# First layer of a hybrid decoder step: another order of the projections, key rows taken earlier, and masks applied by predicated copies

## The chip, the cores and the metric

The kernel runs on one core of one Trainium2 chip, in fp32 throughout. The metric is device time in microseconds (us). A core has five engines that work side by side, each through its own list of instructions in order: TensorE (PE, with its weight loads shown as PEld), VectorE (DVE), ScalarE (ACT), GpSimd (POOL) and SyncE (SP), which here only issues the loads of weights. They wait for one another on semaphores. An instruction that waits holds up everything behind it on its own engine, and this is what the change is about.

## The reference, cut to what matters

The model has two layers and runs for a prompt of 512 tokens and for 8 samples of 4 tokens each; the kernel handles all 544 tokens together. Only the mixer of the first layer is touched by the change:

```python
u = xn @ w_in
q_a, k_a, v_a, g_a, gk_lr, q_b, f_b, i_b, g_b = split(u)
log_alpha = log_sigmoid(gk_lr @ w_gk2 + b_gk) / 16
o_a, _ = chunk_gated_linear(q_a * DK_A ** -0.5, k_a, v_a, log_alpha, s_gla)
log_f = logaddexp(log(max(lb, 1e-20)), log1p(-lb) + log_sigmoid(f_b))
k_b = (1 - lb) * sigmoid(-f_b)
o_b, _ = chunk_gated_linear(silu(q_b) * N_B ** -0.5, k_b, i_b, log_f, s_hgrn)
# in chunk_gated_linear, by chunks of 64 tokens: b = cumsum(log_g)
scores[t, s] = sum_c q[t, c] * k[s, c] * exp(b[t, c] - b[s, c])   # for s <= t
```

Heads 0 to 3 ("a") have 64 key columns and heads 4 to 7 ("b") have 128. Two "a" heads share a tile of 128 rows, so keys, queries and decays make up six tiles: tile 0 and 1 (a pair of "a" heads each), tiles 2 to 5 (one "b" head each).

## The kernel before, in words

**Units.** The projection `xn @ w_in` is computed in 29 units of 128 output columns each (`even_units`, L590), in the order f_b (4 units), gk (1), k_a (2), q_a (2), q_b (4), v_a (4), i_b (4), g_a (4), g_b (4). The text numbers them in the order in which they run, unit 0 to unit 28. A unit is 48 matmuls of 128 x 272 (L328): each fp32 weight is split into a rounded part (w_head) and the rest (w_rest), and each input also, and three of the four products are formed. Units go alternately to slab 0 and slab 1 (two weight buffers, each with its PSUM banks, 0 and 1 or 2 and 3). gk has one unit only, on slab 0, and the unit that follows it is on slab 0 as well.

**Feeding a unit.** SP loads 512 KB of raw weights into a slab (L277), and waits before each load until the slab's earlier rest has been taken (rest_ok). ACT makes w_head (L292) when the load has landed and the slab's previous unit is done (`act_head`), and DVE makes w_rest (L297, `dve_rest`). The helper `ahead` puts the head and the rest of the next unit of the same slab right behind the end of a unit, in ACT's and DVE's lists. SP issues loads strictly in the order of the stages. Before the first norm, ACT and DVE split one slab for each of slab 0 and slab 1, written out by hand in the list `todo` (near L2412), ahead of `norm_part(norm0)`. In the norm, ACT squares eight tiles (L506) and DVE adds them (L534, L537).

**What runs beside the units.** All four engines walk through the units, and after the unit's own work a fixed piece of the decay and score work is written into each engine's list by unit number. `dve_decay` and `act_decay` are chains of steps that yield (logarithms, exponentials, running sums L752 `scan`). `steps_after` says how many of the 36 factor steps are taken after a unit (six tiles, levels 1 to 6): for each, POOL subtracts (L804, L805), ACT takes the exponential (L883), DVE multiplies by keys and queries (L830, L831). There are two buffers for these, so POOL runs at most two steps ahead of DVE. `job_after` says after which unit PE computes a head's scores (`pe_scores`, L913 for the prompt, L918 for the samples): seven levels, and level n waits for factor step n of its tile. Jobs 0 to 7 stand after units 13, 14, 17, 18, 20, 22, 24 and 26.

**Masks.** `masked` on DVE multiplies each level's scores in PSUM by its 0/1 mask and adds the levels up (L848, L853, L856 and, for the samples, L860, L864, L867: 11 instructions for a head). The next job on PE waits for the multiplications, as they free the banks.

**Value rows.** After units 13 to 20, PE transposes the values that the unit made (L620, L621). These transposes stand in the middle of the following unit, and ACT waits for them, copies them out (L643, L645) and only then takes the factor steps of its unit.

**The end.** For each of the six tiles, POOL forms differences to the chunk's last token (L815), ACT two exponentials (L888, L889) and DVE four instructions (L873 to L876, `dve_ends`). All six stand after units 27 and 28, three after each. PE then transposes each tile of keys into rows (L936, L937, `key_rows_even`): three after unit 28 and three at the head of `pe_chunks`, and ACT copies them (L1007, L1009). Behind that come the chunk recurrence (L954 to L969) and the samples' part (L987, L998).

Of the kernel before, what the change touches and what calls it, by code (L numbers as in the profile page):

```python
# [16 lines left out]
F32R = mybir.dt.float32r  # L17
ACT = mybir.ActivationFunctionType
ALU = mybir.AluOpType
# [133 lines left out]
def trunk(nc, a, o, known, seen, stop=99):  # L153
    ctx = ExitStack()
    with ctx:
# [59 lines left out]
        for name, n in (("f_b", 2), ("gk", 1), ("k_a", 1), ("q_a", 1), ("q_b", 2), ("v_a", 2), ("i_b", 2), ("g_a", 2),  # L215
                        ("g_b", 2)):
# [161 lines left out]
        pT = cols(34 * T + 5 * D + 5 * KTILES * P, 8, 5, CE)  # L378
        qk = cols(0, LEVELS, T)
        ee = soft[:, 0:2, :]  # L380
        mt = cols(LEVELS * T, 2, 512)
# [6 lines left out]
        lbs = cols(34 * T + 5 * D + 5 * KTILES * P + 2500, 40)  # L388
# [9 lines left out]
        lvmask = tab[:, 0:7 * CE].rearrange("p (l t) -> p l t", l=7)  # L398
# [177 lines left out]
        def norm_part(n):  # L576
# [3 lines left out]
        norm0 = Norm("mix0", lambda k: col("norm_mix", k), "f_b")  # L580
# [10 lines left out]
                      ("f_b", "gk", "k_a", "q_a", "q_b", "v_a", "i_b", "g_a", "g_b")  # L591
                      for i in range(stages[name][0]) for s in range(len(stages[name][1]))]
        value_tile = {u: u - 13 for u in range(13, 21)}
        job_after = {13: 0, 14: 1, 17: 2, 18: 3, 20: 4, 22: 5, 24: 6, 26: 7}
        steps_after = {10: 2, 11: 2, 12: 2, 15: 3, 16: 3, 18: 1, 19: 5, 20: 1, 21: 5, 22: 1, 23: 5, 24: 1, 25: 5}

        def pe_even_in(pe):
            for u, (name, i, s, last) in enumerate(even_units):
                between = (lambda: value_rows(pe, u - 1)) if u - 1 in value_tile else None
                unit_products(pe, name, i, s, tile_ready(norm0) if u == 0 else None, between=between)  # L600
                if u == 5:
# [9 lines left out]
                if u == 28:  # L611
                    for j in range(3):
                        key_rows_even(pe, j)
# [9 lines left out]
        def act_even_in(act):  # L623
            act.dma_start(wgk2[0:16, :], a["w_gk2"][0]).then_inc(*E1.dma.loaded("wgk2"))
            decay, exps = act_decay(act), act_scores(act)
            for u, (name, i, s, last) in enumerate(even_units):
# [12 lines left out]
                if u in (1, 3, 6, 7, 10, 12, 13, 14):  # L639
# [9 lines left out]
                if u >= 27:  # L649
                    for kt in range(3 * (u - 27), 3 * (u - 27) + 3):  # L650
                        act_ends(act, kt)

        def dve_even_in(dve):
            decay, factor = dve_decay(dve), dve_factors(dve)
            for u, (name, i, s, last) in enumerate(even_units):
# [9 lines left out]
                if u == 5:  # L665
# [4 lines left out]
                if u in (0, 2, 5, 8, 9, 10, 11, 14, 15, 16, 17, 19):  # L670
                    next(decay)
                if u in job_after and u != 26:
# [3 lines left out]
                if u == 26:  # L676
                    masked(dve, job_after[u])
                if u >= 27:
                    for kt in range(3 * (u - 27), 3 * (u - 27) + 3):
                        dve_ends(dve, kt)  # L680
# [6 lines left out]
        zz = lg[:, :, :]  # L687
        hz = lg[:, 2:6, :]

        def dve_decay(dve):  # L690
# [11 lines left out]
            step(dve.tensor_scalar(lb_om, lb, -1.0, 1.0, ALU.mult, ALU.add), "lbo")  # L702
            yield
            for s in range(2):
                dve.wait_ge(bank_free[s], used["k_a"][s])
            dve.wait_ge(*E1.dve.at("z1"))
            step(dve.scalar_tensor_tensor(out=soft, in0=zz, scalar=-1.0, in1=zz, op0=ALU.mult, op1=ALU.max), "abs")
            yield
            dve.wait_ge(*E2.act.at("ln"))
            step(dve.scalar_tensor_tensor(out=soft, in0=zz, scalar=0.0, in1=soft, op0=ALU.min, op1=ALU.subtract), "lsig")  # L710
            yield
            step(dve.tensor_scalar(lg[:, 0:2, :], soft[:, 0:2, :], 1.0 / 16.0, None, ALU.mult), "gla")
            for kt in range(2):
                scan(dve, kt)
            step(dve.tensor_tensor(kk[:, 2:6, :], soft[:, 2:6, :], hz, ALU.subtract), "kz")
            yield
# [15 lines left out]
            for t in range(4):  # L732
                dve.scalar_tensor_tensor(out=lg[:, 2 + t, :], in0=lg[:, 2 + t, :], scalar=lb_c[:, t:t + 1],
                                         in1=soft[:, 2 + t, :], op0=ALU.max, op1=ALU.add).then_inc(
                    *E2.dve.done(f"lf{t}"))
            yield
# [4 lines left out]
            scan(dve, 2)  # L741
            yield
            dve.wait_ge(*E2.act.at("qs"))
            dve.tensor_scalar(qq[:, 2:6, :], qq[:, 2:6, :], NBK ** -0.5, None, ALU.mult).then_inc(*E2.dve.done("qb"))
            for kt in range(3, KTILES):
                scan(dve, kt)
                yield
# [7 lines left out]
        def act_decay(act):  # L755
# [5 lines left out]
            act.activation(lb_1m, lb_om, ACT.Ln).then_inc(*E2.act.done("l1m"))  # L761
            yield
            act.wait_ge(*E2.dve.at("abs"))
            act.activation(soft, soft, ACT.Exp, scale=-1.0).then_inc(*E2.act.done("e"))
            yield
            act.wait_ge(*E2.act.at("e"))
            act.activation(soft, soft, ACT.Ln, bias=1.0).then_inc(*E2.act.done("ln"))
# [6 lines left out]
            yield  # L774
# [19 lines left out]
        def pool_scores(pool):  # L794

            for n, (kt, level) in enumerate(steps):
# [8 lines left out]
                pool.tensor_tensor(e[:, :, 1, :], b[:, :, 1, :], mid, ALU.subtract).then_inc(*E3.pool.done(f"e{n}"))  # L805

            for kt in range(KTILES):
                b, e = lg[:, kt, :], ee[:, kt % 2, :]
                if kt >= 2:
                    pool.wait_ge(*E3.dve.at(f"kh{kt - 2}"))  # L810
                else:
                    pool.wait_ge(*E3.dve.at(f"qk{len(steps) - 2 + kt}"))
                for lo, n, c in ((0, NCE, CE), (TP, NB, ST)):
                    bb = b[:, lo:lo + n * c].rearrange("p (n c) -> p n c", c=c)
                    ins = pool.tensor_tensor(e[:, lo:lo + n * c].rearrange("p (n c) -> p n c", c=c),  # L815
                                             bb[:, :, c - 1:c].to_broadcast([P, n, c]), bb, ALU.subtract)
                ins.then_inc(*E3.pool.done(f"eh{kt}"))

        def dve_factors(dve):
            for s in range(2):  # L820
                dve.wait_ge(bank_free[s], used["q_b"][s])
# [13 lines left out]
        def masked(dve, j):  # L835

            h = jobs[j][1]
            b0 = 4
            dve.wait_ge(*E3.pe.at(f"g{h}"))
            if j > 0:  # L840
                dve.wait_ge(*E3.dve.at(f"ps{jobs[j - 1][1]}"))
            for q in range(4):
                nl = 2 if q < 3 else 1
                out = mt[:, 1, 0:nl * 256] if q else mt[:, 0, 0:512]
                m = lvmask[:, 2 * q:2 * q + nl, :].unsqueeze(2).to_broadcast([P, nl, 4, CE])
                if q > 1:
                    dve.wait_ge(*E3.dve.at(f"a{h}_{q - 1}"))
                dve.tensor_tensor(out.rearrange("p (l c t) -> p l c t", l=nl, c=4),  # L848
                                  ps[:, b0 + q, 0:nl * 256].rearrange("p (l c t) -> p l c t", l=nl, c=4), m,
                                  ALU.mult).then_inc(*E3.dve.done(f"m{h}_{q}"))  # L850
                if q > 0:
                    dve.wait_ge(*E3.dve.at(f"m{h}_{q}"))
                    dve.tensor_tensor(mt[:, 0, 0:nl * 256], mt[:, 0, 0:nl * 256], out, ALU.add).then_inc(  # L853
                        *E3.dve.done(f"a{h}_{q}"))
            dve.wait_ge(*E3.dve.at(f"a{h}_3"))
            dve.tensor_tensor(pT[:, h, 0:4, :], mt[:, 0, 0:256].rearrange("p (c t) -> p c t", c=4),  # L856
                              mt[:, 0, 256:512].rearrange("p (c t) -> p c t", c=4), ALU.add).then_inc(
                *E3.dve.done(f"p{h}"))

            dve.tensor_tensor(mt[0:TS, 1, 0:96].rearrange("p (l t) -> p l t", l=3),  # L860
                              ps[0:TS, b0 + 3, 256:352].rearrange("p (l t) -> p l t", l=3),
                              lvmask[0:TS, 0:3, 0:TS], ALU.mult).then_inc(*E3.dve.done(f"s{h}"))
            dve.wait_ge(*E3.dve.at(f"s{h}"))
            dve.tensor_tensor(mt[0:TS, 1, 0:32], mt[0:TS, 1, 0:32], mt[0:TS, 1, 32:64], ALU.add).then_inc(  # L864
                *E3.dve.done(f"s2{h}"))
            dve.wait_ge(*E3.dve.at(f"s2{h}"))
            dve.tensor_tensor(pT[0:TS, h, 4, 0:TS], mt[0:TS, 1, 0:32], mt[0:TS, 1, 64:96], ALU.add).then_inc(  # L867
                *E3.dve.done(f"ps{h}"))

        def dve_ends(dve, kt):  # L870
            b, e = lg[:, kt, :], ee[:, kt % 2, :]
# [14 lines left out]
        def act_ends(act, kt):  # L886
            act.wait_ge(*E3.pool.at(f"eh{kt}"))
            act.activation(ee[:, kt % 2, :], ee[:, kt % 2, :], ACT.Exp)  # L888
            act.activation(lg[:, kt, :], lg[:, kt, :], ACT.Exp).then_inc(*E3.act.done(f"eq{kt}"))  # L889

        def pe_scores(pe, j):
# [3 lines left out]
            if j == 0:  # L895
                pe.wait_ge(*E1.dve.at("z1"))
                for s in range(2):
                    pe.wait_ge(bank_free[s], used["q_b"][s])
# [3 lines left out]
            for level in range(LEVELS + 1):  # L902
                left = kk[r0:r0 + dk, kt, :] if level == 0 else qk[r0:r0 + dk, level - 1, :]
                right = qq[r0:r0 + dk, kt, :] if level == 0 else left
                if j > 0 and level % 2 == 0:
                    pe.wait_ge(*E3.dve.at(f"m{jobs[j - 1][1]}_{level // 2}"))
                if j > 0 and level == 0:
                    pe.wait_ge(*E3.dve.at(f"s{jobs[j - 1][1]}"))
# [7 lines left out]
                if level <= 2:  # L916
                    at = 256 + 32 * level
                    pe.matmul(ps[0:TS, b0 + 3, at:at + TS], left[:, TP:T], right[:, TP:T], start=True, stop=True)  # L918
# [8 lines left out]
        def key_rows_even(pe, j):  # L927
# [3 lines left out]
            if j < 2:  # L931
                pe.wait_ge(*E3.dve.at(f"ps{HA + HB - 1}"))
# [6 lines left out]
        def pe_chunks(pe):  # L939
            for j in range(3, KTILES):  # L940
                key_rows_even(pe, j)
# [60 lines left out]

        def act_chunks(act):
            for j in range(KTILES):
                b0 = 4 + 2 * (j % 2)
                act.wait_ge(*E4.pe.at(f"kt{j}"))
# [1492 lines left out]
```

## Time and profile before

| | us |
|---|---|
| median of 3 runs (2268.4 to 2269.01) | 2269.0 |
| the profiled execution, its own time | 2277.18 |
| its span, first to last instruction | 2275.2 |
| PE busy | 1958.6 (86%) |
| DVE busy | 991.6 (44%) |
| ACT busy | 747.1 (33%) |
| POOL busy | 158.2 (7%) |

The span is what the profiler sees between the first and the last instruction; the execution's own time is 1.98 us longer, and the unprofiled median is 8.2 us shorter than that. Busy shares are averages over the whole span. In the profile's rows the clock column (PEclk) is TensorE's granted clock as a share of 2.4 GHz: 1.00 is 2.4 GHz, 0.50 is 1.2 GHz. Times in rows count from the span's start.

### The profile page before, as it was taken

The page shows a single profiled execution, that of the slowest core. Times are in us where ns is not written, and L with a number is a line of the kernel's source. Part 1 is how long each engine was busy: PE and PEld are TensorE (multiplying, and loading weights), DVE is VectorE, ACT ScalarE, POOL GpSimd, SP SyncE. Part 2 cuts the span into 40 slices and gives each one's busy share as a digit, 9 for nine tenths or more (in the row PEclk, how much of TensorE's full clock was granted, in tenths as well). Part 3 has the DMA queues.
Part 4 walks back from the last instruction along what each step waited for, and adds up shares of the span by engine and source line. Part 5 has one row for each costly group of instructions (what it writes and reads, how often), then busy time and mean ns, then how long its engine had stood idle before and what let it go on. Part 6 is the DMA issues. An engine that isn't in the chain of part 4 may idle for free.

```text
span 2275.2 us, 48233 instructions
## 1 busy us (share of the span) xinstructions
PE 1958.6 (86%) x21197; PEld 1818.7 (80%) x21197; DVE 991.6 (44%) x1359; ACT 747.1 (33%) x963; POOL 158.2 (7%) x159
## 2 busy tenths in 40 slices
PE   4999989787999999896898867678578999999987
PEld 4998978577999999793787756666358899999976
DVE  5477721344332333547488433323453433323343
ACT  3353320344541222322365121111362442222233
POOL 1043521101000000100000000000100100000010
PEclk8999955588999999997899866755559999999988
DMA  3221220212232233120122200001202223233211
GB/s 99 75 66 48 66 65 8 56 47 91 86 97 79 77 89 99 51 84 19 56 66 57 66 4 4 4 18 27 42 0 74 93 83 100 67 92 90 86 56 49
DMA packets 237103, 138.60 MB, mean 61 GB/s; under 512 B 6561, under 2 KB 232161, under 8 KB 236945
## 3 DMA queue, kind: packets, MB, share of 16 engines
q1 hardware_dynamic: 226528, 114.31, 17.4%
q0 software_dynamic: 4048, 13.67, 2.4%
q10 hardware_dynamic: 6368, 8.22, 1.1%
q8 instruction: 135, 2.21, 0.4%
q14 instruction: 24, 0.19, 0.0%
HBM read 128.02 MB, written 8.16 MB: 60 GB/s over the span
## 4 chain that ended last, share of the span: by engine, by line
PE 76%; DVE 13%; ACT 5%; issue 4%; DMA 1%; POOL 1%; ACTq 0%; DVEq 0%; POOLq 0%
PE ps L328 55%; PE ps L1906 1%; PE ps L1900 1%; DVE mix L527 1%; DVE x_split L547 1%; PE ps L998 1%; PE ps L969 1%; PE ps L959 1%; PE ps L954 1%; PE ps L987 1%; PE ps L1328 1%; ACT w_head L292 1%; PE ps L1526 1%; PE ps L2067 1%; DVE x_split L1577 1%
## 5 line engine op out<-in xcount | busy, mean ns | idle before, releaser
L328 PE MATMUL ps<-x_split,w_head 128*128 128x272 f32 (+1 forms) x5568 | 953.4, 294 | 73.7 <-DVE x_split L547 41.1
L328 PEld LDWEIGHTS ps<-x_split,w_head 128*128 128x128 f32 x5568 | 807.5, 193 | 96.3 <-issue 69.0
L328 PE MATMUL ps<-x_split,w_rest 128*128 128x272 f32 (+1 forms) x2784 | 585.3, 292 | 0.0
L292 ACT ACTIVATE w_head<-w_raw 128x1024 fp32r<-128x1024 f32 (+1 forms) x206 | 228.4, 1109 | 704.8 <-PE ps L328 697.0
L328 PEld LDWEIGHTS ps<-x_split,w_rest 128*128 128x128 f32 x2784 | 446.2, 193 | 0.0
L297 DVE TENSOR_TENSOR w_rest<-w_raw,w_head 128x1024 fp32r<-128x1024 f32 (+1 forms) x206 | 268.2, 1302 | 398.8 <-ACT w_head L292 398.7
L328 PE MATMUL ps<-hidden_split,w_head 128*128 128x272 f32 x1408 | 233.1, 287 | 0.0
L328 PEld LDWEIGHTS ps<-hidden_split,w_head 128*128 128x128 f32 x1408 | 198.0, 188 | 0.0
L328 PE MATMUL ps<-hidden_split,w_rest 128*128 128x272 f32 x704 | 145.2, 287 | 0.0
L1180 DVE TENSOR_TENSOR hT<-hT,ps 128x544 f32 (+1 forms) x48 | 34.7, 722 | 207.9 <-PE ps L328 207.9
L527 POOL TENSOR_TENSOR mix<-hT,mix 128x544 f32<-128x544 f32 x20 | 36.8, 1842 | 1098.6 <-ACT mix L511 1078.2
L328 PEld LDWEIGHTS ps<-hidden_split,w_rest 128*128 128x128 f32 x704 | 110.0, 188 | 0.0
L1296 DVE TENSOR_TENSOR mix<-mix,ps 128x544 f32<-128x544 f32 x44 | 31.8, 723 | 132.1 <-PE ps L328 132.1
L292 ACT ACT_TABLE_LOAD x21 | 26.9, 1283 | 92.5 <-PE ps L328 82.1
L1900 PE MATMUL ps<-odd_quad 32*32 32x32 f32 x2080 | 31.8, 228 | 15.6 <-DVE odd_quad L2024 8.5
L1900 PEld LDWEIGHTS ps<-odd_quad 32*32 32x32 f32 x2080 | 28.7, 141 | 19.6 <-issue 9.5
L804 POOL TENSOR_TENSOR mix<-mix 128x256 f32<-128x256 f32 (+1 forms) x36 | 32.4, 899 | 158.3 <-DVE mix L831 89.5
L913 PE MATMUL ps<-mix 64*64 64x64 f32 (+1 forms) x896 | 36.7, 229 | 7.6 <-DVE mix L831 7.6
L527 DVE TENSOR_TENSOR mix<-hT,mix 128x544 f32<-128x544 f32 x20 | 30.1, 1525 | 26.2 <-ACT mix L511 25.8
L913 PEld LDWEIGHTS ps<-mix 64*64 64x64 f32 (+1 forms) x896 | 30.9, 140 | 11.2 <-DVE mix L831 8.7
L497 DVE TENSOR_TENSOR mix<-mix 128x544 f32<-128x544 f32 x48 | 34.5, 720 | 11.2 <-ACT mix L491 11.2
L517 ACT ACTIVATE x_split<-mix,vectors 128x544 fp32r<-128x544 f32 x40 | 28.3, 744 | 33.2 <-POOL mix L527 28.8
(361 smaller groups left out, 2235.2 us busy)
## 6 DMA issues: line engine op xcount, KB each, us to landing
w_raw<-in_w_ffn_gate SPq DMA_DIRECT2D x44, 512.0 KB, 3.8
w_raw<-in_w_ffn_up SPq DMA_DIRECT2D x44, 512.0 KB, 3.8
w_raw<-in_w_ffn_down SPq DMA_DIRECT2D x32, 704.0 KB, 4.4
w_raw<-in_w_in_even SPq DMA_DIRECT2D x29, 512.0 KB, 3.8
w_raw<-in_w_ple_gate SPq DMA_DIRECT2D x16, 512.0 KB, 3.7
w_raw<-in_w_out_even SPq DMA_DIRECT2D x8, 512.0 KB, 3.7
w_raw<-in_rw_wr SPq DMA_DIRECT2D x8, 512.0 KB, 3.6
w_raw<-in_rw_wk SPq DMA_DIRECT2D x8, 512.0 KB, 3.7
```

The costliest lines, as they stand in the source:

```text
L292: act.activation(wh[:, s, 0:kt * P], raw[:, s, 0:kt * P], ACT.Copy).then_inc(head_ok[s], 1)
L297: dve.tensor_tensor(wl[:, s, 0:kt * P], raw[:, s, 0:kt * P], wh[:, s, 0:kt * P].bitcast(F32), ALU.subtract).then_inc(rest_ok[s], 1)
L328: mm = pe.matmul(ps[:, 2 * s + h, 0:half.stop - half.start], w[:, s, k * P:(k + 1) * P], x[:, k, half], start=first and k == 0, stop=k == ...
L497: dve.tensor_tensor(n.sum, n.sum, n.sq[:, s, :], ALU.add).then_inc(sum_ok, 1)
L517: act.activation(xh[:, k, :], n.y[:, k % 3, :], ACT.Copy, scale=n.gain(k)).then_inc(*s.act.done(f"h{k}"))
L527: eng.tensor_tensor(n.y[:, k % 3, :], hT[:, k, :], n.rs, ALU.mult).then_inc(*signal.done(f"y{k}"))
L547: dve.scalar_tensor_tensor(out=xl[:, k, :], in0=n.y[:, k % 3, :], scalar=n.gain(k), in1=xh[:, k, :].bitcast(F32), op0=ALU.mult, op1=ALU.su ...
L804: pool.tensor_tensor(e[:, :, 0, :], mid, b[:, :, 0, :], ALU.subtract)
L913: mm = pe.matmul(ps[64 * (c % 2):64 * (c % 2) + CE, b0 + level // 2, at:at + CE], left[:, c * CE:(c + 1) * CE], right[:, c * CE:(c + 1) * CE],
L1180: dve.tensor_tensor(h, h, out2(s), ALU.add).then_inc(bank_free[s], 1)
L1296: dve.tensor_tensor(two(prod), two(act_out), out2(1), ALU.mult).then_inc(prod_ok, 1)
L1900: mm = pe.matmul(at_block(out, p, g, j, i), at_block(bT, p, g, j, i), at_block(xx, p, g, j, i), start=True, stop=True)
```

## The change

The new order of the stages is gk, k_a, q_a, f_b, q_b, and from there as before. The first two tiles' decay is computed on its own, ahead of the "b" decays; the lists by unit number are rewritten; the work of the end stands in the lists of earlier units, in buffers of its own (`ends`); key rows are transposed after units 23, 24 and 25. The masks become integers, and ten predicated copies write a head's scores into pT, which POOL sets to zero once.

```diff
@@ stages and even_units @@
-        for name, n in (("f_b", 2), ("gk", 1), ("k_a", 1), ("q_a", 1), ("q_b", 2), ("v_a", 2), ...
+        for name, n in (("gk", 1), ("k_a", 1), ("q_a", 1), ("f_b", 2), ("q_b", 2), ("v_a", 2), ...
@@ buffers @@
+        ends = soft[:, 2:4, :]
-        mt = cols(LEVELS * T, 2, 512)
-        lvmask = tab[:, 0:7 * CE].rearrange("p (l t) -> p l t", l=7)
+        lvmask = tab.bitcast(I32)[:, 0:7 * CE].rearrange("p (l t) -> p l t", l=7)
@@ lists by unit @@
-        job_after = {13: 0, 14: 1, 17: 2, 18: 3, 20: 4, 22: 5, 24: 6, 26: 7}
-        steps_after = {10: 2, 11: 2, 12: 2, 15: 3, 16: 3, 18: 1, 19: 5, 20: 1, 21: 5, 22: 1, 23: 5, 24: 1, 25: 5}
+        job_after = {6: 0, 7: 1, 10: 2, 11: 3, 15: 4, 17: 5, 19: 6, 21: 7}
+        ends_after = {15: 0, 17: 1, 19: 2, 21: 3, 22: 4, 23: 5}
+        steps_after = {4: 2, 5: 4, 7: 1, 8: 2, 9: 3, 13: 2, 14: 4, 15: 1, 16: 5, 17: 1, 18: 5, 19: 1, 20: 5}
+        keys_after = {23: (0, 1), 24: (2, 3), 25: (4, 5)}
@@ pieces of act_decay and dve_decay, by unit @@
-                if u in (1, 3, 6, 7, 10, 12, 13, 14):            # ACT
+                if u in (1, 3, 9, 11, 12, 13):
-                if u in (0, 2, 5, 8, 9, 10, 11, 14, 15, 16, 17, 19):   # DVE
+                if u in (0, 2, 3, 4, 8, 10, 11, 12, 13, 14, 15, 17):   # and 9, behind its factor steps
@@ dve_decay: the first pair alone, in the pieces of units 2, 3, 4 @@
+            dve.wait_ge(*E1.dve.at("z1"))
+            step(dve.scalar_tensor_tensor(out=soft[:, 0:2, :], in0=gz, ...), "absg")
+            yield
+            dve.wait_ge(*E2.act.at("lng"))
+            step(dve.scalar_tensor_tensor(out=soft[:, 0:2, :], in0=gz, ...), "lsigg")
+            step(dve.tensor_scalar(gz, soft[:, 0:2, :], 1.0 / 16.0, None, ALU.mult), "gla")
+            scan(dve, 0)
+            yield
+            scan(dve, 1)
@@ act_decay, in the piece of unit 3 @@
+            act.activation(soft[:, 0:2, :], soft[:, 0:2, :], ACT.Exp, scale=-1.0).then_inc(*E2.act.done("eg"))
+            act.wait_ge(*E2.act.at("eg"))
+            act.activation(soft[:, 0:2, :], soft[:, 0:2, :], ACT.Ln, bias=1.0).then_inc(*E2.act.done("lng"))
@@ pool_scores @@
+            pool.memset(pT_flat, 0.0).then_inc(*E3.pool.done("zero"))
...
+                if level == LEVELS and kt >= 2:
+                    pool_ends(pool, kt - 2)
@@ masked @@
+            for level in range(3):
+                dve.copy_predicated(pT[0:TS, h, 4, 0:TS], lvmask[0:TS, level, 0:TS], ps[0:TS, 7, at:at + TS])
+            for level in range(LEVELS + 1):
+                dve.copy_predicated(pT[:, h, 0:4, :], lvmask[:, level, :].unsqueeze(1).to_broadcast([P, 4, CE]),
+                                    ps[:, 4 + level // 2, at:at + 256].rearrange("p (c t) -> p c t", c=4))
@@ pe_scores @@
-                if level <= 2:
-                    pe.matmul(ps[0:TS, b0 + 3, at:at + TS], left[:, TP:T], right[:, TP:T], start=True, stop=True)
+            for level in range(3):
+                mm = pe.matmul(ps[0:TS, b0 + 3, at:at + TS], left, right, start=True, stop=True)
@@ todo, ahead of the first norm @@
-            dict(scalar=lambda e: [act_head(e, "f_b", s, 0) for s in range(2)],
-                 vector=lambda e: [dve_rest(e, "f_b", s, 0) for s in range(2)]),
+            dict(scalar=lambda e: [act_head(e, "gk", 0, 0), act_head(e, "k_a", 1, 0)],
+                 vector=lambda e: [dve_rest(e, "gk", 0, 0), dve_rest(e, "k_a", 1, 0)]),
```

## Rows read from the trace of the kernel before

**Rows 1.** Stretches: the units, then the gap before the chunks

```profile
core 0: us, PE busy (x) PEld busy (x) DVE busy (x) ACT busy (x) POOL busy (x), PEclk, DMA share, GB/s
39.79:282.94 243.15, 230.18 (x2379) 222.15 (x2379) 162.72 (x247) 95.75 (x127) 72.84 (x81) 0.95 0.23 62
282.94:298.06 15.12, 5.85 (x33) 4.55 (x31) 10.38 (x20) 10.07 (x23) 12.04 (x15) 0.67 0.53 135
```

**Rows 2.** The chain in order of time: start, length, what

```profile
21.45 2.36 DVE w_rest L297 x2
...
48.10 25.09 PE ps L328 x198
```

**Rows 3.** SP's loads in order of time

```profile
22.70 0.37 SPq L277 DMA_DIRECT2D w_raw<-in_w_in_even  x1
63.62 0.99 SPq L277 DMA_DIRECT2D w_raw<-in_w_in_even  x2
```

**Rows 4.** What PE waited for, 50 to 300: total, times, longest

```profile
PE ps L936 <- DVE mix L873: 8.2, 1, 8.2
PE ps L913 <- DVE mix L831: 7.6, 8, 1.7
PE ps L328 <- DVE w_rest L297: 3.0, 1, 3.0
```

**Rows 5.** What PE waited for, 216 to 283 (jobs 5 to 7)

```profile
PE ps L913 <- DVE mix L831: 2.9, 3, 1.2
```

**Rows 6.** ACT in order of time (in brackets: idle before)

```profile
69.31 1.06 ACT L292 ACTIVATE w_head<-w_raw 128x1024 fp32r<-128x1024 f32 x1 [6.97 <-DMA w_raw<-in_w_in_even]
...
99.37 1.28 ACT L767 ACT_TABLE_LOAD   x1
...
119.14 2.02 ACT L770 ACTIVATE mix<-mix 128x2176 f32<-128x2176 f32 x1
```

**Rows 7.** DVE in order of time: decay steps, masks of job 0

```profile
113.87 2.48 DVE L752 TENSOR_TENSOR_SCAN mix<-tables,mix 128x544 f32<-128x544 f32 x2
116.27 2.80 DVE L715 TENSOR_TENSOR mix<-mix 128x2176 f32<-128x2176 f32 x1
...
120.57 2.50 DVE L719 TENSOR_SCALAR mix<-mix 128x544 f32<-128x544 f32 x4
...
140.25 1.28 DVE L848 TENSOR_TENSOR mix<-ps,tables 128x512 f32<-128x512 f32 x2
...
143.74 0.42 DVE L848 TENSOR_TENSOR mix<-ps,tables 128x256 f32<-128x256 f32 x1
...
145.49 0.18 DVE L867 TENSOR_TENSOR mix<-mix 32x32 f32<-32x32 f32 x1
```

**Rows 8.** POOL in order of time: the first factor step, its second half

```profile
116.75 2.83 POOL L805 TENSOR_TENSOR mix<-mix 128x272 f32<-128x272 f32 x1
```

**Rows 9.** PE in order of time: scores of jobs 3 and 4

```profile
189.91 0.68 PE L913 MATMUL ps<-mix 64*64 64x64 f32 x16
...
192.27 2.08 PE L913 MATMUL ps<-mix 64*64 64x64 f32 x64
207.61 0.69 PE L913 MATMUL ps<-mix 128*64 128x64 f32 x16
...
214.68 0.69 PE L913 MATMUL ps<-mix 128*64 128x64 f32 x16 [1.71 <-DVE mix L831]
```

**Rows 10.** ACT in order of time: value rows, then factor steps

```profile
205.46 0.60 ACT L643 ACTIVATE mix<-ps 128x512 f32<-128x512 f32 x1 [2.73 <-PE ps L621]
...
206.11 1.17 ACT L883 ACTIVATE mix<-mix 128x544 f32<-128x544 f32 x2
```

**Rows 11.** Stretches behind jobs 0 and 4, then the chunk stage

```profile
137.80:144.70 6.90, 6.88 (x53) 6.57 (x54) 6.47 (x11) 4.45 (x4) 3.63 (x4) 0.51 0.47 131
...
216.20:219.80 3.60, 3.60 (x18) 3.60 (x18) 3.46 (x7) 0.00 (x0) 0.64 (x1) 0.53 0.52 146
304.50:377.50 73.00, 71.27 (x336) 66.13 (x336) 11.48 (x42) 4.78 (x8) 0.00 (x0) 0.50 0.00 1
377.50:438.00 60.50, 57.56 (x184) 41.23 (x184) 14.68 (x12) 4.79 (x6) 17.59 (x14) 0.50 0.22 59
```

More of the change, by code:

```diff
@@ L214, in trunk @@
         X = (xh, xl)
-        for name, n in (("f_b", 2), ("gk", 1), ("k_a", 1), ("q_a", 1), ("q_b", 2), ("v_a", 2), ("i_b", 2), ("g_a", 2),
+        for name, n in (("gk", 1), ("k_a", 1), ("q_a", 1), ("f_b", 2), ("q_b", 2), ("v_a", 2), ("i_b", 2), ("g_a", 2),
                         ("g_b", 2)):
@@ L610, in pe_even_in @@
                     pe_scores(pe, job_after[u])
-                if u == 28:
-                    for j in range(3):
-                        key_rows_even(pe, j)
+                for j in keys_after.get(u, ()):
+                    key_rows_even(pe, j)
         def value_rows(pe, u):
@@ L648, in act_even_in @@
                     next(exps)
-                if u >= 27:
-                    for kt in range(3 * (u - 27), 3 * (u - 27) + 3):
-                        act_ends(act, kt)
+                if u in ends_after:
+                    act_ends(act, ends_after[u])
+                for j in keys_after.get(u, ()):
+                    act_key_rows(act, j)
         def dve_even_in(dve):
@@ L675, in dve_even_in @@
                     next(factor)
[L676 to L680, printed above, removed]
+                if u == 9:
+                    next(decay)
+                if u in ends_after:
+                    dve_ends(dve, ends_after[u])
         gam = vec[:, 0, VCOL["hgrn_gamma"][1]:VCOL["hgrn_gamma"][1] + 4]
         lb_e, lb_r, lb_sm, lb, lb_c, lb_1m, lb_om, lb_t = (lbs[:, 4 * i:4 * i + 4] for i in range(8))
-        zz = lg[:, :, :]
+        gz = lg[:, 0:2, :]
         hz = lg[:, 2:6, :]
@@ L735, in dve_decay @@
                     *E2.dve.done(f"lf{t}"))
+            scan(dve, 2)
             yield
@@ L740, in dve_decay @@
                     *E2.dve.done(f"kb{t}"))
-            scan(dve, 2)
-            yield
             dve.wait_ge(*E2.act.at("qs"))
             dve.tensor_scalar(qq[:, 2:6, :], qq[:, 2:6, :], NBK ** -0.5, None, ALU.mult).then_inc(*E2.dve.done("qb"))
-            for kt in range(3, KTILES):
-                scan(dve, kt)
-                yield
+            yield
+            scan(dve, 3)
+            yield
+            scan(dve, 4)
+            yield
+            scan(dve, 5)
+            yield
         def scan(dve, kt):
@@ L837, in masked @@
             h = jobs[j][1]
-            b0 = 4
             dve.wait_ge(*E3.pe.at(f"g{h}"))
[L840 to L854, printed above, removed]
@@ L863, in masked @@
[L863 to L868, printed above, removed]
+            if j == 0:
+                dve.wait_ge(*E3.pool.at("zero"))
+            for level in range(3):
+                at = 256 + 32 * level
+                if level > 0:
+                    dve.wait_ge(*E3.dve.at(f"s{h}_{level - 1}"))
+                dve.copy_predicated(pT[0:TS, h, 4, 0:TS], lvmask[0:TS, level, 0:TS],
+                                    ps[0:TS, 7, at:at + TS]).then_inc(
+                    *E3.dve.done(f"s{h}_{level}"))
@@ L870, in dve_ends @@
+            for level in range(LEVELS + 1):
+                at = (level % 2) * 256
+                if level > 0:
+                    dve.wait_ge(*E3.dve.at(f"m{h}_{level - 1}"))
+                dve.copy_predicated(pT[:, h, 0:4, :], lvmask[:, level, :].unsqueeze(1).to_broadcast([P, 4, CE]),
+                                    ps[:, 4 + level // 2, at:at + 256].rearrange("p (c t) -> p c t", c=4)).then_inc(
+                    *E3.dve.done(f"m{h}_{level}"))
         def dve_ends(dve, kt):
-            b, e = lg[:, kt, :], ee[:, kt % 2, :]
+            b, e = lg[:, kt, :], ends[:, kt % 2, :]
@@ L887, in act_ends @@
             act.wait_ge(*E3.pool.at(f"eh{kt}"))
-            act.activation(ee[:, kt % 2, :], ee[:, kt % 2, :], ACT.Exp)
+            act.activation(ends[:, kt % 2, :], ends[:, kt % 2, :], ACT.Exp)
             act.activation(lg[:, kt, :], lg[:, kt, :], ACT.Exp).then_inc(*E3.act.done(f"eq{kt}"))
@@ L905, in pe_scores @@
                 if j > 0 and level % 2 == 0:
-                    pe.wait_ge(*E3.dve.at(f"m{jobs[j - 1][1]}_{level // 2}"))
-                if j > 0 and level == 0:
-                    pe.wait_ge(*E3.dve.at(f"s{jobs[j - 1][1]}"))
+                    pe.wait_ge(*E3.dve.at(f"m{jobs[j - 1][1]}_{min(level + 1, LEVELS)}"))
                 if level:
@@ L939, in pe_chunks @@
         def pe_chunks(pe):
-            for j in range(3, KTILES):
-                key_rows_even(pe, j)
             for s in range(2):
```

94 lines of the change are left out of this document (46 added, 48 removed).

## The prediction

> **What bounds the kernel now.** I read the chain of waits first, in order of time: up to the end of the units it runs almost only through the projection's matmuls, four units in 25.09 us, so 6.0 us a unit [rows 2]. The changed stretch is thus bound by PE, and an edit counts only where it changes a wait of PE or its clock. The stretches give the sizes: 243.15 us for the 29 units with all that stands between them, and then 15.12 us before the first chunk in which PE works 5.85 us [rows 1]. The list of PE's waits names the holes: 8.2 us before the key rows, 7.6 us in eight waits for factor steps, 3.0 us for a weight's rest [rows 4]. The granted clock is the rest: it drops to half behind job 0 and job 4 and stays at half through the chunk and sample stage although PE is busy for 71.27 of 73.00 us there [rows 11].
>
> **The start: +7.0.** ACT and DVE must split one slab each for gk (slab 0) and k_a (slab 1) before the first norm. Now both slabs' loads go out at once, and the two rests run from 21.45 to 23.81, on the chain [rows 2]. In the new order SP has gk's load, then k_a's for slab 0, then k_a's for slab 1. The middle one waits until gk's rest has been taken, and the third stands behind it in SP's queue. So slab 1's load is issued only after gk's rest, near 22.7, where SP issues its next load today [rows 3]. A pair issued from 63.62 let ACT's head start at 69.31, 5.7 us later [rows 3, 6]. So: head 28.4 to 29.5, rest to 30.7, and only then squares and sums, since both engines' lists are in order. 30.8 instead of 23.8 is +7.0, with the whole norm behind it. Nothing covers it: PE has no input yet. The bounds are 0 and 7.5. The 3.0 us wait for the next rest on the same slab [rows 4] moves from behind unit 4 to behind unit 0 and stays.
>
> **Jobs 0 to 3: +10.9.** I pass the new lists by hand with durations of now: 1.06 an ACT head, 1.28 a table load, 2.0 an exponential or logarithm of four tiles (1.1 of two) [rows 6], 1.2 a DVE rest and a scan, 1.3 a two-tile decay step, 2.8 the subtraction before the second exponential [rows 2, 7]. A job without waits takes 4.4 us [rows 9]. A factor step takes 1.7 when two are under way (five steps from ACT's start at 206.11 to the last scores at 214.68) [rows 9, 10]; the very first takes longer, as POOL ends it 4.5 us after its scan [rows 7, 8].
> Job 0, after unit 6, counted from the end of unit 3: ACT's head, three table loads, logarithms and exponential end at 7.7, DVE's steps and scan 0 at 11.1. DVE then has the rest for unit 6, which is ready at 13.2, so unit 6 starts 1.2 late and ends at 19.2. The first step is done at 16.2, DVE's own work of unit 5 (copy and rest, 2.0) comes between, the six are done at 26, and the job at 27.2 where 23.6 would be free: 3.6 + 1.2, against 0.3 now, +4.5.
> Job 2, after unit 10, from the end of unit 9: copy, head, exponential, table load, logarithm, table load and the first exponential of the steps end at 8.9; three steps are done at 13, the job at 14.2, where 10.4 would be free: 3.8. Now it has 2.0 (the 7.6 less 2.9 in jobs 5 to 7 and less some 2.7 in job 4) [rows 4, 5], so +1.7 or a little more; I take 1.7.
> Job 3, after unit 11: behind these steps DVE has the logarithm's combination (2.4), a rest (1.3) and then, in one piece, the subtraction and eight scalings (2.8 + 2.2 + 1.7), and only then job 2's masks. The first banks come free at 25, unit 11 ends at 20.2: +4.7, where there is no wait now. Bounds for the three together: 0, if steps are ready, and 16.
>
> **Jobs 4 to 7: +7.3.** Job 4 now is the pattern: ACT can take the steps only after the value rows from the middle of the next unit (205.46), and the job takes 7.8 us from 207.61, 3.3 over the free one [rows 9, 10]. Jobs 5, 6 and 7 stand after g_a and g_b units now, without value rows, and have 2.9 us of waits together [rows 5]. Moved to units 17, 19 and 21 they all get job 4's pattern, with five steps taken one unit earlier: 3 x 3.3 - 2.9 = +7.0. The samples' matmuls move behind the last level, so behind the last wait: +0.3. Bounds 0 and 10.
>
> **Masks: 0.** A head's masks take 5.4 us of DVE now, from 140.25 to 145.67 [rows 7]. No row shows a predicated copy. From below it is 0.31 us for 128 x 256 (half of one of the four scalings of 544 elements, 2.50 / 4, with no fixed cost), from above 0.84, twice the multiplication with a mask (0.42), if it reads its target besides [rows 7]; I take 0.46 with its wait, as the multiplication from PSUM with a mask of the same size (143.74), and 0.22 for the three small ones (145.49) [rows 7]. That is 7 x 0.46 + 0.66 = 3.9, 1.5 less for each head. But DVE's masks end before ACT releases the steps in jobs 4 to 7, so this is hidden; where it isn't (job 3) it stands in the sum. POOL's clearing of pT lies under its idle time before the first step. If masks were all on the path, they would give 8 x 1.5 = 12.
>
> **The end: -10.6.** The 15.12 us go [rows 1], as POOL, ACT and DVE do the ends beside units 15 to 23. What PE did in them stays: 5.85 us busy at mean clock 0.67 is 3.9 us at full clock. ACT's copy of the last tile (0.6) stays in front of the chunks. 15.1 - 3.9 - 0.6 = 10.6. Bounds 8 and 11.
>
> **Clock: +3.4 and -5.0.** Each slow stretch behind a job with waits costs half of its length, 1.7 us for the 3.6 us behind job 4 [rows 11]. Four jobs (3, 5, 6, 7) newly get such waits; I take two, +3.4, bounds 0 and 10. At the chunks the clock is now slow from the start, after the 8.2 us hole. Behind units without a hole it will be full at first: behind job 4's first score it lasted 8.6 us (207.61 to 216.2). At full clock PE does twice the work, so t us of it save t: I take 5.0, bounds 0 and 8.6.
> The Trainium skill (TensorE: Matmul & The Clock Gate, Part 1) says that the halved clock is the default and that sustained activity lifts it. By it a chunk stage entered without a hole would stay at full clock. The trace disagrees so far: busy throughout, it was never lifted [rows 11].
>
> **Sum.** 7.0 + 10.9 + 7.3 + 3.4 - 10.6 - 5.0 = +13.0. The profiled execution (2277.2, span 2275.2) would become 2290; the median is 8.2 below the profiled one, so 2269.0 + 13.0 = 2282.
>
> **Rivals.** (A) The end decides. The steps keep up and no job waits longer than now: 7.0 - 10.6 - 5.0 = -8.6, 2260. For it: DVE is busy for only 162.7 of 243 us [rows 1]. Against: the waits are of order, not of load. It decides as soon as the jobs' added waits with their clock stay under 8.6 us. (B) The masks' 12 us are on the path: 13.0 - 12 = +1, 2270. For it: DVE does masks before factor steps in its list. Against: in jobs 4 to 7 ACT releases the steps later than DVE has done the masks [rows 10]. (C) A predicated copy takes the upper bound, 0.84: 7 x 0.42 = 2.9 more for each head, on the path behind three of them, +8.8, 2291. Nothing speaks against it but its small operands. (D) The clock stays full from the chunks to the samples: 128.8 us of busy PE at half [rows 11] would be 64 shorter, instead of 5: 2223. It needs that the 8.2 us hole ahead of the chunks is what holds the clock down.
>
> **Chances.** Forecast 0.55 (its own range 2275 to 2291), A 0.20, B 0.12, C 0.10, D 0.03. I count 0.2% (4.5 us) as what a measurement tells from no change: slower is the forecast and C, 0.65; same is B, 0.12; faster is A and D, 0.23. The range leaves out D, half of what could lie beyond C and the far end of A: 2258 to 2292.
>
> **What would show it.** ACT's second head at 28 us instead of 13 and the first sum at 31 (start). PE waits for factor steps of some 25 us in all, and waits inside jobs 5, 6 and 7 of 2 us or more each. PE waiting for DVE's masks at job 3. No wait before the key rows, the first chunk under 1 us behind the last unit, at about 310 us. A clock of 1.00 for the first 3 to 9 us of the chunks. The prediction is wrong if the first chunk starts before 300 us, if the start isn't delayed, or if anything behind the chunks changes by more than 2 us.

## The result, and the profile after

The changed kernel takes 2289.2 us (median of 4 runs, 2288.07 to 2290.44) against 2269.0 for the kernel before on the same chip: a ratio of 1.0073, 95% interval [1.0055, 1.0091], so 20 us slower. The forecast was 2282, 13 slower. The profiled execution took 2290.44 us, its span 2288.7, which is 13.5 more than before. The two differences are not the same, since the profiled execution of the kernel before was 8.2 us above its median and that of the changed kernel only 1.2; on another chip the kernel before ran between 2261.7 and 2277.4 us. Of all executions in this document one, of the kernel with the early ends alone, took 2528 us at a mean clock of 0.69 and is left out of its ratio.

What PE waited for from 50 to 330 us (total, times, longest), to be held against [rows 4]:

```profile
PE ps L919 <- DVE mix L853: 19.9, 18, 2.1
PE ps L329 <- DVE w_rest L298: 4.0, 2, 3.0
PE ps L919 <- DVE mix L874: 1.9, 1, 1.9
PE ps L960 <- issue: 0.8, 1, 0.8
```

The 8.2 us before the key rows are gone. The waits for factor steps (L913 before, L919 now) have gone from 7.6 us in 8 waits to 19.9 in 18, and a wait for masks (L874) is new. The same view of single stretches says where: 2.3 us in job 0, 2.8 in job 2, 4.4 in job 4 and 10.4 in jobs 5 to 7 (this row is of 209 to 300 us; [rows 5] had 2.9 in 3):

```profile
PE ps L919 <- DVE mix L853: 10.4, 9, 1.6
```

PE in order of time, job 5 and the start of the chunks. Each of jobs 5, 6 and 7 has these three waits, as job 4 had in the kernel before [rows 9]:

```profile
213.79 2.08 PE L919 MATMUL ps<-mix 128*64 128x64 f32 x64
217.31 0.69 PE L919 MATMUL ps<-mix 128*64 128x64 f32 x16 [1.44 <-DVE mix L853]
218.47 0.69 PE L919 MATMUL ps<-mix 128*64 128x64 f32 x16 [0.48 <-DVE mix L853]
220.71 1.12 PE L919 MATMUL ps<-mix 128*64 128x64 f32 x16 [1.55 <-DVE mix L853]
...
317.94 1.74 PE L960 MATMUL ps<-mix 64*64 64x128 f32 x16 [0.76 <-issue]
```

The stretches answer to [rows 11]; the columns are those of [rows 1], the clock the one before the last two:

```profile
55.60:62.40 6.80, 5.50 (x24) 5.53 (x25) 1.27 (x2) 0.00 (x0) 0.00 (x0) 0.50 0.58 154
103.40:110.20 6.80, 5.66 (x51) 5.29 (x52) 6.52 (x14) 1.58 (x2) 4.11 (x5) 0.50 0.17 39
140.90:147.70 6.80, 5.68 (x59) 5.15 (x55) 5.59 (x6) 2.09 (x3) 0.99 (x2) 0.50 0.00 0
154.60:164.80 10.20, 10.20 (x135) 10.02 (x134) 8.85 (x17) 1.41 (x1) 0.00 (x0) 0.50 0.19 54
192.10:202.30 10.20, 7.75 (x84) 7.06 (x79) 8.86 (x14) 2.72 (x4) 8.82 (x10) 0.50 0.22 59
219.40:226.20 6.80, 5.49 (x39) 5.34 (x40) 5.96 (x10) 1.63 (x3) 5.42 (x6) 0.50 0.29 77
243.30:250.10 6.80, 5.84 (x41) 5.69 (x42) 5.99 (x13) 1.28 (x2) 4.09 (x6) 0.50 0.29 80
267.20:274.00 6.80, 6.03 (x42) 5.88 (x43) 6.03 (x14) 2.18 (x4) 2.70 (x3) 0.50 0.31 81
317.94:321.80 3.86, 3.86 (x40) 3.57 (x40) 2.42 (x7) 3.83 (x3) 3.86 (x6) 1.00 0.59 149
321.80:394.00 72.20, 70.48 (x332) 65.50 (x328) 11.47 (x42) 6.79 (x9) 6.30 (x5) 0.50 0.18 44
```

The first eight are slow stretches of 6.8 or 10.2 us, 61.2 us in all: one around the 3.0 us wait for a weight's rest behind unit 0, the others around and behind jobs with waits (0, 2, 3, 4, 5, 6 and 7). The kernel before had 20.4 us of them in its units: the two of [rows 11], one of 3.4 us from 76.2 behind its wait for a rest, and one behind job 2 that [rows 11] leaves out:

```profile
178.70:185.50 6.80, 5.34 (x35) 5.25 (x36) 6.20 (x8) 1.62 (x3) 2.92 (x4) 0.50 0.27 77
```

The chunk stage of the changed kernel has full clock for its first 3.86 us and half clock from then on.

The start, in the order of each engine. First SP, then ACT, then DVE; before, ACT's second head was at 13.14 and the sums began at 24.27:

```profile
20.55 1.01 SPq L278 DMA_DIRECT2D w_raw<-in_w_in_even  x2
```

```profile
26.27 1.06 ACT L293 ACTIVATE w_head<-w_raw 128x1024 fp32r<-128x1024 f32 x1 [13.66 <-DMA w_raw<-in_w_in_even]
```

```profile
19.29 1.22 DVE L298 TENSOR_TENSOR w_rest<-w_raw,w_head 128x1024 fp32r<-128x1024 f32 x1
27.35 1.22 DVE L298 TENSOR_TENSOR w_rest<-w_raw,w_head 128x1024 fp32r<-128x1024 f32 x1 [6.83 <-ACT w_head L293]
29.03 5.70 DVE L539 TENSOR_TENSOR mix<-mix 128x544 f32<-128x544 f32 x7
```

The account of the two profiles, from starts of PE's instructions: unit 0 starts 4.8 us later (43.06, before 38.29); from there to the end of unit 28 it is 274.1 us instead of 244.7, +29.4; the gap to the chunks is 0.8 instead of 15.1, -14.3; so the chunks start 19.9 us later (317.94, before 298.06). At the output projection behind the chunk stage 16.5 are left (494.06, before 477.53), as the chunks had full clock for 3.9 us. From there on nothing was changed, and 3.1 us are given back. PE's own time says where the 29.4 us are: its busy time in the units is 246.9 us (before 231.7), its idle time 27.2 (before 13.0).

### The profile page after: what moved, and what is told of

The parts are those of the page before. It is cut to its first block, busy times and chain, and to the rows that moved or that the text cites. A ratio compares the mean times of both kernels' runs of the same rounds, so it can differ in the third digit from the quotient of the medians.

```text
span 2288.7 us, 48219 instructions
## 1 busy us (share of the span) xinstructions
PE 1959.5 (86%) x21197; PEld 1821.3 (80%) x21197; DVE 981.2 (43%) x1353; ACT 748.1 (33%) x967; POOL 160.5 (7%) x160
## 4 chain that ended last, share of the span: by engine, by line
PE 71%; DVE 11%; ACT 4%; issue 3%; DMA 1%; POOL 1%; ACTq 0%; DVEq 0%; POOLq 0%
PE ps L329 51%; PE ps L1913 1%; PE ps L1907 1%; PE ps L1004 1%; PE ps L975 1%; PE ps L965 1%; DVE x_split L549 1%; DVE mix L529 1%; PE ps L960 1%; PE ps L993 1%; PE ps L1335 1%; PE ps L1533 1%; DVE x_split L1584 1%; PE ps L1889 1%; PE ps L2074 1%
## 5 line engine op out<-in xcount | busy, mean ns | idle before, releaser
L919 PE MATMUL ps<-mix 64*64 64x64 f32 (+1 forms) x896 | 39.6, 252 | 22.2 <-DVE mix L853 19.9
L919 PEld LDWEIGHTS ps<-mix 64*64 64x64 f32 (+1 forms) x896 | 35.4, 162 | 26.2 <-DVE mix L853 23.0
L570 PE MATMUL ps<-mix,ones 128*128 128x272 f32 x28 | 12.1, 570 | 36.3 <-DVE mix L499 20.3
```

The source lines that it names most:

```text
L919: mm = pe.matmul(ps[64 * (c % 2):64 * (c % 2) + CE, b0 + level // 2, at:at + CE], left[:, c * CE:(c + 1) * CE], right[:, c * CE:(c + 1) * CE],
```

## The experiments

The groups of kernels that ran together shared their runs of the kernel before: 2272.7 us for the first group, 2271.4 for the second, 2270.6 for the third. Each group ran on a chip of its own, so kernels of different groups are compared by their ratios to the kernel before.

### The changed kernel again

> The changed kernel once more. The unprofiled medians differ by 20.2 us, the two profiled spans by 13.5 us. If the difference lies in one disturbed or lucky profile of the kernel before, this one again shows 2288 to 2291 us and the same trace: units' end near 317 us, chunks' first score at 318 us. If the changed kernel itself varies with where its waits fall, the profile differs by several us from the first.

Measured: 2289.5 us, ratio 1.0083 [1.0054, 1.0111]. The profile has the chunks at 313.6 us, 4.4 earlier, with the same waits (20.0 and 2.1 us): the slow stretch behind job 3 is missing and others are shorter, 47.6 us of them instead of 61.2. So neither theory held as written: the waits repeat, and the granted clock behind them varies from run to run, by some 4 us in this stretch.

### The start

```diff
-                for s, (w, c, step, row, kt, _) in enumerate(units):
+                for s, (w, c, step, row, kt, _) in (reversed(list(enumerate(units))) if name == "k_a" else enumerate(units)):
```

> The changed kernel, with SP's two loads of k_a in the other order: slab 1 first, which waits for nothing. Theory (the start's delay comes from SP's queue: slab 1's load stands behind one that waits for gk's rest): ACT's second head at 13 us instead of 28, first sum near 24 instead of 31, and the whole kernel 6 to 7 us shorter, near 2282. Rival (the time is given back in a later wait or in the clock): the start is 7 us earlier, but the end by under 3 us.

Measured: 2284.9 us, 1.0053 [1.0034, 1.0072], 4.6 less than the changed kernel on the same chip, where 6 to 7 were expected. The intervals overlap, but the trace is plain: the second head is back at 13 us, where its load has landed, and the squares start at 21.23.

```profile
13.04 1.06 ACT L293 ACTIVATE w_head<-w_raw 128x1024 fp32r<-128x1024 f32 x1 [0.17 <-DMA w_raw<-in_w_in_even]
21.23 1.20 ACT L508 ACTIVATE mix<-hT 128x544 f32<-128x544 f32 x2 [7.13 <-DVE vectors L468]
```

The delay was SP's order. It was 5.0 us at unit 0 (43.06 against 38.08) and not 7.0. The way from a load to its head was forecast rightly: issued at 20.55, head at 26.27, 5.7 us. But gk's rest was done by 20.51 and not by 22.7, as PE had its inputs at 11.68 instead of 13.08 us. This goes with the number of slab loads that SP issues at once: with one in front (six profiles, the changed kernel's among them) PE's first instruction starts between 11.33 and 11.71 us, with two (eight profiles, this one at 12.90) between 12.04 and 13.08.

### Where ACT takes the steps

```diff
+                early = min(2, steps_after.get(u, 0)) if u in (14, 16, 18, 20) else 0
+                for _ in range(early):
+                    next(exps)
                 if u in value_tile:
                     act.wait_ge(*E1.pe.at(f"vt{t}"))
```

> The changed kernel, with ACT taking the first two of the factor steps of units 14, 16, 18 and 20 ahead of its wait for the value rows, the others behind it as now. Theory (jobs 4 to 7 wait since ACT releases the steps only after the value rows): PE's waits inside jobs 5, 6 and 7 fall from 3.5 us each to under 1.5, the slow-clock stretch behind each shrinks or goes, 8 to 14 us less in all, near 2278. Rival (the three engines' round trip of a step is what binds, wherever ACT starts): waits stay above 3 us each, and the time within 2 us of the changed kernel's.

Measured: 2279.7 us, 1.0031 [1.0015, 1.0048], 9.9 less than the changed kernel, and the intervals are apart. PE's waits from 205 to 290 us, against 10.4 in 9 above:

```profile
PE ps L922 <- DVE mix L856: 5.2, 6, 1.6
```

Half of the waits of jobs 5 to 7 went, and each slow stretch behind them fell from 6.8 to 3.4 us (this is behind job 7):

```profile
260.20:263.60 3.40, 3.40 (x30) 3.22 (x26) 3.18 (x7) 1.11 (x3) 1.63 (x2) 0.50 0.18 39
```

So the value rows bind jobs 5 to 7. What stays, 1.7 us for each (the theory had under 1.5), is a wait further up: ACT now stands idle for POOL's differences, 1.73 us ahead of the last step of job 5. Job 4 did not gain: its waits are 4.4 us with and without the early steps. In the changed kernel ACT waits there for POOL, not for value rows, and between DVE's steps stand a rest and a scan:

```profile
191.19 0.63 ACT L891 ACTIVATE mix<-mix 128x512 f32<-128x512 f32 x1 [2.53 <-POOL mix L822]
```

### Jobs 4 to 7 where they were

```diff
-        job_after = {6: 0, 7: 1, 10: 2, 11: 3, 15: 4, 17: 5, 19: 6, 21: 7}
+        job_after = {6: 0, 7: 1, 10: 2, 11: 3, 20: 4, 22: 5, 24: 6, 26: 7}
-        ... 13: 2, 14: 4, 15: 1, 16: 5, 17: 1, 18: 5, 19: 1, 20: 5}
+        ... 18: 1, 19: 5, 20: 1, 21: 5, 22: 1, 23: 5, 24: 1, 25: 5}
-        keys_after = {23: (0, 1), 24: (2, 3), 25: (4, 5)}
+        keys_after = {27: (0, 1), 28: (2, 3, 4, 5)}
```

> The changed kernel with jobs 4 to 7 and their steps where they were before (after units 20, 22, 24, 26), ends and key rows accordingly after units 20 to 28; the new order, jobs 0 to 3 and the masks stay. Theory: the waits of jobs 5, 6, 7 go back to about 1 us each and their slow stretches go, 8 to 14 us less than the changed kernel, near 2278; the start's 7 us and the waits of jobs 0 to 3 stay, so it is not faster than the kernel before by more than 3 us. Rival (the steps bind as much beside g_a's units): within 3 us of the changed kernel.

Measured: 2280.6 us, 1.0040 [1.0026, 1.0054], about 9 less than the changed kernel, as the theory had it. The chunks start at 301.74 us, in a profile of the fastest of its 11 executions. The waits of jobs 4 to 7 are still 8.2 us in 7 (14.8 in the changed kernel, 5.5 before; job 4 has its value rows), and those of jobs 5 to 7 are 1.6 to 2.0 each instead of the expected 1. But behind them only two slow stretches are left, of 6.8 and 3.4 us.

### Job 2's masks ahead of the decay piece

```diff
+                if u == 10:
+                    masked(dve, job_after[u])
                 if u in (0, 2, 3, 4, 8, 10, 11, 12, 13, 14, 15, 17):
                     next(decay)
-                if u in job_after:
+                if u in job_after and u != 10:
```

> The changed kernel, with DVE doing job 2's masks ahead of the long decay piece of unit 10 instead of behind it. Theory (job 3 waits because the masks stand behind that piece): the wait before job 3 (1.9 us) goes, but DVE's pieces behind come later by up to the masks' 3.4 us and job 2's own end, so at most 4 us less, near 2286. Rival (DVE's decay chain is what sets job 4): job 4's wait grows by as much as job 3's falls, and the time stays within 1 us.

Measured: 2283.6 us, 1.0047 [1.0031, 1.0063]. The wait for masks is gone, and job 4's waits stay (4.6 us, 4.4 in the changed kernel), so it was the order of masks and decay piece. 5.9 less is more than the 1.9 us and than the 4 of the theory, though the intervals overlap; the slow stretch behind job 3 (10.2 us in the first profile) is absent here, but it was absent in the second profile of the changed kernel too, so the clock's share in this is not settled.

### The masks alone, in either order

The two kernels exchange the predicated copies for the multiplications and additions of before, or the other way, each with its order of the samples' matmuls:

```diff
-                dve.tensor_tensor(out.rearrange("p (l c t) -> p l c t", l=nl, c=4), ps[...], m, ALU.mult)
...
+                dve.copy_predicated(pT[:, h, 0:4, :], lvmask[:, level, :].unsqueeze(1).to_broadcast([P, 4, CE]), ps[...])
```

> The kernel before with the predicated copies alone: the masks and the samples' matmuls behind the levels as in the changed kernel, every list and the order as before. Theory (masks are beside PE's path in most jobs): DVE's masks 1.5 us shorter for each head, the time at most 5 us less, near 2268 to 2272 on a chip where the kernel before takes 2272. Rival (the masks are on the path: DVE does them ahead of the factor steps for which PE waits): the waits inside jobs 4 to 7 and the slow clock behind job 4 go, 8 to 12 us less, near 2262.

> The changed kernel with the multiplications and additions of before in place of the predicated copies, and the samples' matmuls between the levels as before. Theory: DVE has 1.5 us more for each head, which shows where DVE is behind (jobs 1 to 3) and hides where ACT releases the steps (jobs 4 to 7): 0 to 6 us longer than the changed kernel, 2290 to 2296. Rival (masks on the path everywhere): 12 us longer or more, above 2301.

Measured: the old order with copies 2274.3 us, 1.0006 [0.9993, 1.0019], no change. The new order with old masks 2289.4, 1.0064 [1.0040, 1.0087], as the changed kernel. A predicated copy of 128 x 256 takes 0.444 us (mean of 56 in the changed kernel), the multiplication of that size 0.42 [rows 7]:

```profile
L874 DVE COPY_PREDICATED mix<-tables,ps 128x256 f32<-128x256 int32 x56 | 24.8, 444 | 1.6
```

In the new order two effects cancel. DVE is free sooner: with old masks job 3's wait is 6.2 us instead of 1.9. And the samples' matmuls come behind the last wait: with old masks, and these matmuls between the levels, jobs 5 to 7 wait 2.5 us each instead of 3.5, and all waits for steps are 14.7 us instead of 19.9. In the old order only the second is seen. Job 5 there with the copies:

```profile
229.84 3.04 PE L900 MATMUL ps<-mix 128*64 128x64 f32 x96
234.58 0.69 PE L900 MATMUL ps<-mix 128*64 128x64 f32 x16 [1.70 <-DVE mix L834]
235.19 0.38 PE L907 MATMUL ps<-mix 128*32 128x32 f32 x6
```

PE reaches the last level sooner and waits 1.70 us there instead of 0.75, and then does 0.38 us that formerly filled the wait. PE's waits for steps rose from 7.6 to 12.9 us in that kernel, and no job's waits fell; in its profile the chunks start at 299.51 instead of 298.06 us, but have full clock for the first 2 us, and the output projection starts within 0.2 us of before.

### The early ends alone, in the old order

```diff
+        ends_after = {20: (0,), 22: (1,), 24: (2,), 26: (3,), 27: (4, 5)}
+        keys_after = {27: (0, 1), 28: (2, 3, 4, 5)}
```

> The kernel before with the early ends alone: ends of tiles 0 to 3 after units 20, 22, 24 and 26, of 4 and 5 after unit 27, key rows after units 27 and 28, in buffers of their own; order, jobs, steps and masks as before. Theory (the 8.2 us hole ahead of the key rows goes; the clock stays full into the chunks): 8 to 13 us less. Rival (DVE has no room for it beside old masks in units 20 to 26, so the jobs' waits grow by as much as the hole shrinks): under 4 us less. Should the clock stay full through the chunk stage once there is no hole, it would be 60 us less.

Measured: 2267.5 us, 0.9977 [0.9964, 0.9990]: 4 us less than the kernel before by the medians, 5 by the ratio. That is between the theory (8 to 13) and its rival (under 4). Its profile has the chunks at 288.81 instead of 298.06, of which 1.5 us is an earlier unit 0. PE's waits from 50 to 300 us:

```profile
PE ps L921 <- DVE mix L839: 10.1, 11, 1.6
PE ps L328 <- DVE w_rest L297: 3.0, 1, 3.0
PE ps L944 <- ACT mix L1014: 1.3, 1, 1.3
PE ps L960 <- ACT mix L1014: 1.0, 1, 1.0
```

The hole of 8.2 us went, 2.5 us of it came back as waits for steps, and the key rows behind unit 28 keep 2.3 us. The clock is low in the chunk stage none the less. Together with the changed kernel, where 0.8 us stands ahead of the chunks and full clock lasts 3.86 us, this puts rival D out.

### Put together

Three kernels in the old order with early ends: ACT's two early steps at unit 19; with that, steps split two and four; and then with copies, level 6 copied first so that bank 7 is free for the samples' matmuls between the levels. The fourth is the new order with everything mended.

```diff
-        ... 18: 1, 19: 5, 20: 1, 21: 5, 22: 1, 23: 5, 24: 1, 25: 5}
+        ... 18: 2, 19: 4, 20: 2, 21: 4, 22: 2, 23: 4, 24: 2, 25: 4}
-            for level in range(LEVELS + 1):
+            for pos, level in enumerate((6, 0, 1, 2, 3, 4, 5)):
```

> The kernel before with early ends, and ACT taking two of the steps of unit 19 ahead of the value rows. Theory (job 4's waits come from the value rows): job 4's waits and the slow stretch behind it go, 3 to 5 us less than with early ends alone, so 9 to 13 us less than the kernel before. Rival (another wait takes its place): as with early ends alone, 5 us less.

> The same, with two factor steps behind units 18, 20, 22 and 24 and four behind units 19, 21, 23 and 25, instead of one and five. Theory (a job waits because five round trips of a step do not fit in one unit): the waits of jobs 5 to 7 go, 2 to 4 us less than without the split. Rival (DVE's rest for the next unit now stands behind one more step and PE waits for the weights): no gain or up to 3 us longer.

> The same with the split, with predicated copies (level 6 first), and the samples' matmuls between the levels as before. Theory: with the samples' matmuls back between the levels the copies cost PE nothing, and DVE is free 1.5 us sooner for each head: within 3 us of the version with multiplications, 0 to 3 us shorter. Rival (the copies themselves lengthen a wait of PE): 2 us longer or more.

> The changed kernel's order and copies, with all that was found mended: slab 1 loaded first, job 2's masks ahead of the decay piece, jobs 4 to 7 after units 20 to 26 with steps split two and four, ACT's two steps ahead of the value rows, samples' matmuls between the levels. Theory (the new order itself costs only the waits of jobs 0 and 2): 2262 to 2270 where the kernel before takes 2272, 3 to 6 us above the same mending in the old order. Rival (the new order has a cost that none of these steps holds): above 2274.

| kernel | us | ratio to the kernel before | steps waited for by PE, us |
|---|---|---|---|
| early ends, ACT's early steps | 2264.0 | 0.9967 [0.9950, 0.9984] | 8.8 |
| and steps split | 2263.1 | 0.9961 [0.9944, 0.9978] | 7.7 |
| and copies, samples between levels | 2259.4 | 0.9942 [0.9925, 0.9959] | 5.2 |
| new order, mended | 2260.6 | 0.9950 [0.9933, 0.9967] | 7.2 |

The third is 11 us faster than the kernel before and, on other chips, 30 faster than the changed one. Of single steps among the first three only their sum is clear (0.9942 [0.9925, 0.9959] against 0.9977 [0.9964, 0.9990] for the early ends alone); the intervals of neighbours overlap. The traces say more of each. ACT's early steps took job 4's waits from 2.5 to 1.2 us and its slow stretch away, as the theory had it. The split moved the waits of jobs 5 to 7 only from 5.6 to 5.1 us, so the theory that they would go failed. The copies came out 3.7 us shorter with 2.5 us less of waits, within the intervals. The mended new order came out better than expected and equals the third within the intervals. So the new order of the projections by itself costs or gives less than these intervals resolve, some 4 us; where the jobs, steps and loads stand makes the 30 us.

## Why the prediction was right, step by step

The direction, the order of size and most of the mechanisms were right: 13.0 us forecast, 20.2 measured by the medians, 16.5 in the profiles at the output projection. Part of this is luck: the jobs' waits were priced 3.2 us too high and the clock in the units 8.0 too low, beyond its own bounds of 0 to 10, and these errors offset each other in part.

- **Start, +7.0 forecast, +4.8 found.** The mechanism was right (the load behind a waiting load). The size was off since gk's rest came 2.2 us sooner, which I had not counted: one slab load less stands beside the inputs' own load. The fourteen profiles agree with this.
- **Jobs 0 to 3, +10.9 forecast, +5.7 found.** PE waits 3.3 us at job 0 (1.0 for a rest and 2.3 for steps, forecast 1.2 and 3.6), 2.8 at job 2 (forecast 3.8) and 1.9 at job 3 (forecast 4.7), which is 8.0 us of waits; 0.3 and 2.0 are subtracted for before as I did. At job 3 the mechanism was right, as the experiment with the masks ahead of the decay piece shows. The size was off on both sides: that piece ran in 6.2 us instead of 6.7, with POOL idle beside it, and PE came later, as unit 11 took 7.5 us instead of 6.0 with half clock until 147.7.
- **Jobs 4 to 7, +7.3 forecast, +9.3 found.** 14.8 us of waits against 5.5. Jobs 5 to 7 took job 4's pattern, 3.5 us each where 3.3 was forecast, and two experiments confirm the cause for them. Job 4 itself went from 2.6 to 4.4 us, which was not forecast; ACT waits for POOL there, and no experiment separates why.
- **Masks, 0.** 0 in both orders. The price of a copy was right (0.444 for 0.46 with its wait). The samples' matmuls cost more than the 0.3 that I gave them: 1.0 us of waits in each of jobs 5 to 7.
- **End, -10.6 forecast, -11.0 found.** The gap fell by 14.3, of which the key rows' 3.3 came back beside units.
- **Clock, +3.4 forecast in the units, some +11 found.** This is the term of the sum that was most mis-sized. From unit 0 to unit 28 there are +29.4 us: 3.3 of key rows and 14.7 of waits (22.8 less 8.1) leave 11.4 for the clock. PE's busy time gives the same: 15.2 us more, less 3.3 of key rows, is 11.9. I had counted two new slow stretches of 3.6 us at half their length; there are 40.8 us more of slow clock, which cost under a third of their length. One reason for the lower price is in the rows: six projection matmuls take 1.52 us at half clock and 0.76 at full, but sixteen 64x64 scores 0.88 and 0.50, and part of each stretch is waiting. And the premise that a slow stretch needs a job with waits was too narrow: in the kernel before, job 0 had no wait at all and the clock fell behind it.
- **Clock at the chunks, -5.0 forecast, -3.4 found**, since full clock lasted 3.9 us.

With these sizes the sum is 4.8 + 14.7 + 11.4 - 11.0 - 3.4 = 16.5, as the profiles have it at the output projection. Rival A fell: the added waits with their clock, 26 us, are far above the 8.6 from which it decides. B and C fell by the masks' experiments (copies alone gave nothing where B wanted 12 us, and one takes 0.444 us, not 0.84), D by the chunk stage of every run. Of 20 us in the medians some 4 are not in the profiles; this stays open, within the spread of the kernel before. One sign of being wrong did show, a change behind the chunks of more than 2 us: behind the output projection the profiles differ by 3.1 us. It was set too tight, as that unchanged part differs by up to 6.6 us between the profiles.

## What to carry to other kernels

When a load moves in a strictly ordered queue, ask what the load in front of it waits for, and which engines stand in order behind the one that waits for it. When work is packed closer between matmuls, price its round trip over all engines against the slot it gets, not the engines' loads: DVE was busy about 60% of this stretch and was still what PE waited for. And where the clock falls around the waits, price it from all slow stretches of the trace, not from one of them: here it cost 11 us beside 14.7 us of waits.

## What the runs showed of the hardware

The clock falls behind short 64- and 128-row scores even without idle time: in the kernel before PE was busy 3.79 of the 3.80 us of job 0 ahead of 137.8, and the clock was at half from there to 144.7 [rows 11]:

```profile
134.00:137.80 3.80, 3.79 (x90) 3.19 (x91) 2.41 (x5) 3.79 (x5) 2.84 (x4) 0.99 0.18 42
```

In the chunk stage it stays at half through 72 us in which PE is busy 70.48 us. The same waits (20 us) came with 61.2 and 47.6 us of slow stretches in two profiles of one kernel, and the chunks started 4.4 us apart. The unchanged part behind the chunk stage took between 1791.9 us (2254.9 - 463.0) and 1798.5 us (2262.8 - 464.3) in the profiles, so single profiles of this kernel compare whole times to some 7 us only.
